# The down projection of two feed-forward blocks in seven block products instead of eight, with the affine steps on VectorE

## What is computed

```python
def _swiglu(u, w_gate, w_up, w_down):          # u 1024x1024, w_gate and w_up 1024x2816, w_down 2816x1024
    return (jax.nn.silu(u @ w_gate) * (u @ w_up)) @ w_down

def sublayer(h, j, fn, resid_w):               # shift, scale, gate: rows of mods, from c
    u = (_layer_norm(h) * (1.0 + scale) + shift).astype(h.dtype)
    z = DEEPNORM_ALPHA * h.astype(jnp.float32) + resid_w * gate * fn(u)
    return (_layer_norm(z) * ln_g[layer, j] + ln_b[layer, j]).astype(h.dtype)
```

## Time and profile before

| | us |
|---|---|
| median of 3 runs | 2212.14 (2208.69 to 2212.39) |
| the profiled execution | 2212.68 |
| its span, first to last instruction | 2210.9 |
| PE busy | 2034.5 (92%) |
| DVE busy | 1097.4 (50%) |
| ACT busy | 756.2 (34%) |
| POOL busy | 469.2 (21%) |

### The profile page before, as it was taken

How to read it: one execution, slowest core, us unless ns; L and a number is a source line. 1 busy time by engine, 2 the same in 40 slices (tenths; PEclk the granted TensorE clock), 3 DMA queues, 4 the chain that set the end, 5 groups by cost and what they waited for, 6 DMA issues and landing times. The chain is left out here.

```text
span 2210.9 us, 27004 instructions
## 1 busy us (share of the span) xinstructions
PE 2034.5 (92%) x10350; PEld 1588.2 (72%) x10350; DVE 1097.4 (50%) x1893; ACT 756.2 (34%) x1267; POOL 469.2 (21%) x336
## 2 busy tenths in 40 slices
PE   3999999999999928999889997876999999999997
PEld 2777777777888827676567775665888888878885
DVE  4854444544347483444434445567644444343656
ACT  2533323333223233434423334226433333332331
POOL 0622222220004041000023221242522222100041
PEclk7999999999999969999999999897999999999998
DMA  7253444444743122111032220604122212265341
GB/s 261 79 162 124 157 140 152 136 151 141 286 154 143 58 86 95 39 48 48 11 79 57 48 57 16 232 0 153 62 91 81 91 61 90 88 256 181 143 176 44
DMA packets 157617, 247.47 MB, mean 112 GB/s; under 512 B 8097, under 2 KB 106673, under 8 KB 157361
## 3 DMA queue, kind: packets, MB, share of 16 engines
q1 hardware_dynamic: 126370, 211.36, 27.4%
q10 hardware_dynamic: 30096, 30.25, 4.4%
q0 software_dynamic: 1024, 4.13, 1.2%
HBM read 205.09 MB, written 40.63 MB: 111 GB/s over the span
## 5 line engine op out<-in xcount | busy, mean ns | idle before, releaser
L1280 PE MATMUL f_ps<-f_uh,f_ops 128*128 128x512 f32 x2496 | 795.3, 396 | 9.1 <-DVE acc L1119 4.9
L1280 PEld LDWEIGHTS f_ps<-f_uh,f_ops 128*128 128x128 f32 x2496 | 471.3, 189 | 138.1 <-issue 28.0
L1280 PE MATMUL f_ps<-f_ul,f_ops 128*128 128x512 f32 x1248 | 491.5, 394 | 0.0
L1380 PE MATMUL f_ps<-f_wdh,f_hdh 128*128 128x512 f32 x704 | 274.1, 389 | 0.0
L1380 PE MATMUL f_ps<-f_wdl,f_hdh 128*128 128x512 f32 x704 | 273.9, 389 | 0.0
L1380 PE MATMUL f_ps<-f_wdh,f_hdl 128*128 128x512 f32 x704 | 273.9, 389 | 0.0
L1280 PEld LDWEIGHTS f_ps<-f_ul,f_ops 128*128 128x128 f32 x1248 | 235.8, 189 | 48.4
L1180 DVE TENSOR_TENSOR f_wdl<-f_wd,f_wdh 128x2048 fp32r<-128x2048 f32 x44 | 107.2, 2436 | 227.7 <-ACT f_wdh L1010 227.7
L868 POOL TENSOR_TENSOR f_sums<-f_raw 128x512 f32<-128x512 f32 x80 | 108.0, 1350 | 443.5 <-DVE f_ops L1080 341.2
L1080 DVE TENSOR_TENSOR f_ops<-f_sums,f_ops 128x512 fp32r<-128x512 f32 x160 | 117.7, 735 | 154.0 <-ACT f_ops L906 154.0
L1010 ACT CAST f_wdh<-f_wd 128x2048 fp32r<-128x2048 f32 x44 | 83.9, 1907 | 302.4 <-PE f_ps L1380 258.7
(11 more groups left out here) (214 smaller groups left out, 2671.7 us busy)
## 6 DMA issues: line engine op xcount, KB each, us to landing
f_wd<-in_ffn_w_down SPq DMA_DIRECT2D x44, 1024.0 KB, 4.9
f_raw<-in_ffn_w_gate SPq DMA_DIRECT2D x22, 1024.0 KB, 5.5
f_raw<-in_ffn_w_up SPq DMA_DIRECT2D x22, 1024.0 KB, 5.4
f_hidden<-acc SPq DMA_DIRECT2D x88, 256.0 KB, 2.2
f_hd<-f_hidden SPq DMA_DIRECT2D x44, 512.0 KB, 5.6
f_aw<-in_w_ada ACTq DMA_DIRECT2D x28, 512.0 KB, 3.5
acc<-in_w_ada ACTq DMA_DIRECT2D x28, 512.0 KB, 3.5
in_raw<-in_w_in SPq DMA_DIRECT2D x24, 512.0 KB, 3.8
```

What stands on the lines that cost most here:

```text
L1280: done = nc.tensor.matmul(ps[:, bank, :], l[:, k, :], r[:, k, :], start=fresh and k == 0 and m == 0, stop=closed and k == HK - 1 and m == ...
L1380: done = nc.tensor.matmul(ps[:, b, :], l[n % 3][:, c, P * t:P * t + P], r[n % 3][:, c, NB * (b % 2):NB * (b % 2) + NB], start=p == 0 and c ...
```

## The change

The down product is done in seven block products as well. The tokens are split into halves, and so are the output columns and, pair by pair, the hidden rows. A stage r is one block product summed over the 11 pairs (KD = 11), so there are ND = 77 steps, each with 12 matmuls: 4 token tiles by 3. Step n is pair n % 11 of stage n // 11. The stages are: 0 A11 by B11, 1 A12 by B21, 2 S2 by T2, 3 S1 by T1, 4 S4 by B22, 5 S3 by T3, 6 A22 by T4. Eight banks hold two sets of four tiles (`X_BANKS`, `Y_BANKS`), and a running sum is copied out by ScalarE where two stages share it (`copy_out`).

The sums of hidden blocks S1 to S4 are made by GpSimd in `mix_hidden`, four instructions for each pair, beside the gate and up products, and stored beside A11, A12, A22. The sums of weight blocks T1 to T3 are made by GpSimd in `mix_weights`, three for each pair, while stages 0 and 1 run. T4 is made in `fourth`, during stages 2 and 3, where stage 3 brings the block B21 once more. T3 is split early, beside stage 4 (`third_hi`, `third_lo`), so that a step of stage 5 splits only the hidden block.

Loads are 256 KB blocks in six slots; the parts lie in a ring of four (`DRING`), and those of the last steps also in four extra pairs. The last LAST = 8 steps go by tile, one tile at a time. The gate, residual, statistics, normalising, gain and shift all stand on VectorE, with the normalising fused into the gain (`affine`: two instructions of 128x1024 for tiles 0 to 3 behind steps 64 to 67, four of 128x512 for tiles 4 to 7). ScalarE's normalising and GpSimd's gain and shift are gone.

```diff
-LAST = 3
+KD = PAIRS
+ND = 7 * KD
+DSLOT = 6
+DRING = 4
+LAST = 8
...
+X_BANKS, Y_BANKS = (0, 1, 2, 6), (3, 4, 5, 7)
...
+            def load_mixed(e):
+                k = e // 2
+                if k >= 4:
+                    sp.wait_ge(tw, 3 * (k - 4) + 3)
+                if e % 2 == 0:
+                    load_down(mem.t1[k], 0, 1, k).then_inc(tw_ld[k % 4], 16)
                 else:
+                    load_down(mem.t3[k], 1, 1, k).then_inc(tw_ld[k % 4], 16)
...
+            for n in range(DSLOT, ND):
+                sp.wait_ge(d_lo, n - DSLOT + 1)
+                if stage(n - DSLOT)[0] == 3:
+                    sp.wait_ge(t4_done, stage(n - DSLOT)[1] + 1)
                 load_hidden(n)
+                load_weight(n)
+                if n < DSLOT + 2 * KD:
+                    load_mixed(n - DSLOT)
+                if n == 8:
+                    store_sums(PAIRS - 1)
...
+            def mix_hidden(q):
+                pool.wait_ge(pr, 4 * q + 4)
+                pool.wait_ge(p_st[2], 16 * (q + 1))
+                nc.gpsimd.tensor_tensor(prod(2), prod(1), prod(2), ALU.add).then_inc(mixed, 1)
...
+            def mix_weights(k):
+                t1, t2, t3 = one(mem.t1[k]), one(mem.t2[k]), one(mem.t3[k])
+                pool.wait_ge(tw_ld[k % 4], 32 * (k // 4 + 1))
+                pool.wait_ge(d_lo, k + 1)
+                nc.gpsimd.tensor_tensor(t3, t3, t1, ALU.subtract).then_inc(tw, 1)
+                pool.wait_ge(tw, 3 * k + 1)
+                nc.gpsimd.tensor_tensor(t1, t1, t2, ALU.subtract).then_inc(tw, 1)
+                pool.wait_ge(tw, 3 * k + 2)
+                nc.gpsimd.tensor_tensor(t2, t3, t2, ALU.add).then_inc(tw, 1)
...
+            def fourth(k):
+                n = 3 * KD + k
+                pool.wait_ge(d_ld[n % DSLOT], landed(n))
+                pool.wait_ge(tw, 3 * k + 3)
+                pool.wait_ge(d_lo, 2 * KD + k + 1)
+                nc.gpsimd.tensor_tensor(one(mem.t2[k]), one(mem.slots[n % DSLOT] + 1), one(mem.t2[k]),
+                                        ALU.subtract).then_inc(t4_done, 1)
...
+            def down_hi(n):
+                r, k = stage(n)
+                if later(n) >= DRING:
+                    act.wait_ge(d_mm, steps_done(n - 2 * DRING))
+                elif later(n) >= 0:
+                    act.wait_ge(d_mm, steps_done(5 * KD + 7))
+                elif n >= DRING:
+                    act.wait_ge(d_mm, steps_done(n - DRING))
...
+                act.wait_ge(d_ld[n % DSLOT], landed(n))
+                if r in (2, 3):
+                    act.wait_ge(tw, 3 * k + (3, 2)[r - 2])
+                if r == 6:
+                    act.wait_ge(t4_done, k + 1)
+                nc.scalar.copy(high_of(n), operands(n)).then_inc(d_hi, 1)
...
+            for n in range(2, ND):
+                down_lo(n)
+                for r in (1, 4, 5):
+                    if n == KD * (r + 1) + 2:
+                        for t in range(4):
+                            add_up(r, t)
+                    if n == KD * (r + 1) + 3:
+                        if r == 1:
+                            dve.wait_ge(g_half, 1)
+                        for t in range(4):
+                            weigh(r, t)
+                if 0 <= n - 4 * KD - 1 < KD:
+                    third_lo(n - 4 * KD - 1)
+                if n in (36, 37):
+                    for t in (2 * (n - 36), 2 * (n - 36) + 1):
+                        dve.wait_ge(h_ld[t], 16)
+                        residual(1, t)
...
+                if 64 <= n < 68:
+                    affine(n - 64, 1)
+                if n == 70:
+                    for t in range(4):
+                        dve.wait_ge(h_ld[4 + t], 16)
+                        residual(5, t)
+                if n == 71:
+                    for t in range(4):
+                        dve.wait_ge(d_out, 8 + t + 1)
+                        lv.half(dve, acc[:, 4 + t, :], 4 + t, 1)
...
             def down(n, tiles):
...
+                for t in tiles:
...
+                    for m in range(3):
+                        done = nc.tensor.matmul(ps[:, bank(r, t), :], left[m][:, x, P * t:P * t + P],
...
+            for n in range(ND - LAST):
+                down(n, range(4))
+            for t in range(4):
+                for n in range(ND - LAST, ND):
+                    down(n, (t,))
```

More of the change, by code:

```diff
@@ L598, in __init__ @@
             m.sb(tag + "_space", [P, D])
-        self.small = m
-        at_small, m.end = m.end, m.end + (672 if ada else 1344)
         at_l = m.end - base
@@ new lines, in store_sums, with load_hidden @@
+            def store_sums(q):
+                for n, x in enumerate((2, 1, 0, 3)):
+                    sp.wait_ge(mixed, 4 * q + n + 1)
+                    sp.dma_start(hid[(S2, S3, S1, S4)[x], q], prod(x)).then_inc(sum_st[x], 16)
+            def load_hidden(n):
+                r, k = stage(n)
+                x = (0, 3, 0, 2, 3, 1, 2)[r]
+                sp.wait_ge((p_st if r in (0, 1, 6) else sum_st)[x], 16 * (k + 1))
+                sp.dma_start(one(mem.slots[n % DSLOT]), hid[DOWN_A[r], k]).then_inc(d_ld[n % DSLOT], 16)
```

433 lines of the change are left out of this document (250 added, 183 removed).

## The result

| | median us (lowest to highest, runs) |
|---|---|
| before | 2212.26 (2208.69 to 2213.91, 4) |
| after | 2155.69 (2155.3 to 2156.83, 4) |
| ratio | 0.9745 [0.9731, 0.976] |

The forecast was 2178 us, 2154 to 2202. The direction was right and the time lies just inside the range; the gain is 56.6 us where 34 were forecast.

The account below looks back on a forecast made before the run. The prediction took TensorE's number of matmuls to bound the down product. Its terms, -29.9 + 8 + 8 + 2 - 3.5 - 1.6, gave -17.0 us per FFN, -34 for two: 2178 us, range 2154 to 2202.

Parts of the forecast that it names:

- matmuls: Down product: 132 fewer matmuls per FFN at an unchanged price of 0.227 us, 29.9 us off.
- GpSimd against VectorE: Stages 0 to 3: exclusive lock on the shared SBUF port makes TensorE wait, 8 us per FFN, bounds 0 and 14.
- VectorE's crowd at the end: Steps 64 to 76: 34.3 us of VectorE work in 26.0 us, costing 8 us per FFN, bounds 4 and 10.
- clock: TensorE's clock falls behind about three larger waits in each FFN: 2 us lost, bounds 0 and 5.
- tail: Behind the last down matmul: VectorE's remaining work falls from 12.7 to 9.2 us, 3.5 us less.
- entry: Ahead of the down product: `combine` starts earlier behind a shorter first split, 1.6 us off.
- gate and up otherwise: Gate and up products: hidden-block stores and GpSimd's `mix_hidden` beside them were costed at nothing.
- the crowd at step 24 to 26: Splits, side work and seven 1.29 us port waits: 17.2 us against 12.6 us, a TensorE wait of 4.6 us.
- The ledger of 118.5 against 114.3 us: Port work of GpSimd and VectorE up to step 42 against the time of 42 steps: short by 4.2 us.
- rival 4: Clock stays at the lower level through the waits, matmuls at half speed, 19 us per FFN lost; chance 0.02.
- Rival 3 (DMAs): Loads in stages 0 and 1 don't keep up; at 200 GB/s +9.5 us per FFN, 2231 us; chance 0.04.
- rival 1: Port costs little and clock nothing: 27 us per FFN gained, 2158 us; chance 0.15.

Follow-up runs that it names:

- experiment 5: Kernel after with GpSimd's `mix_weights` and `fourth` on 32 of 512 columns, so most weight sums are left out; 2148.6 us, ratio 0.9713.
- Experiments 6: Kernel after without the eight 128x1024 `affine` instructions of tiles 0 to 3 (gain and shift left out); 2152.5 us, ratio 0.9729.
- 11: Kernel after with side work spread and moved earlier (2147.8 us), plus stage 5's twelve weights, residuals and moments behind split 76; 2144.1 us, ratio 0.9691.
- experiments 1: Kernel before with only the small tables moved behind the large blocks of FFN memory, as in the kernel after; 2203.7 us, ratio 0.9958.
- 4: Kernel before with the gap of its small buffers made 1024 and 2048 bytes in place of 672 and 1344; 2205.4 us, ratio 0.9965.
- experiments 7: Kernel after with tiles 0 to 3 normalised on ScalarE and gain and shift on GpSimd, as before the change; 2168.1 us, ratio 0.9799.
- 12: Kernel after with side work spread and moved earlier (2147.8 us), plus only stage 5's four moments behind split 76; 2144.4 us, ratio 0.9693.

## Why the prediction was right, and what it mis-sized

Per FFN, mean of the two, with the measured value behind what the sum had:

| term | forecast | measured | from |
|---|---|---|---|
| matmuls | -29.9 | -29.9 | 132 fewer at the same price |
| GpSimd against VectorE | +8 | +3.2 | experiment 5, clock loss included |
| VectorE's crowd at the end | +8 | +8.4 | 217.8 (experiment 5) less 239.3 - 29.9, clock loss included |
| clock | +2 | in the two above | |
| tail | -3.5 | -3.4 | 12.7 to 9.3 |
| entry | -1.6 | -1.6 | wait 2.46 to 0.9 |
| gate and up otherwise | 0 | -4.9 | 6.45 less 1.6 |
| sum | -17.0 | -28.2 | |

**Matmuls, entry, tail** came out as worked out. The price stood: in the down product of after a matmul away from waits starts 0.227 us behind the one before.

**The port was the term that failed: 8 us for 3.2.** The mechanism is right: experiment 5 removes the wait with the work. The Trainium skill's exclusive lock (SBUF — State Buffer, section "SBUF: two separate sides") agrees in kind. GpSimd and then VectorE in order of time, kernel after:

```profile
576.07 1.29 POOL L994 TENSOR_TENSOR f_blocks<-f_blocks 128x512 f32<-128x512 f32 x1
577.43 2.15 POOL L996 TENSOR_TENSOR f_blocks<-f_blocks 128x512 f32<-128x512 f32 x1
```

```profile
576.18 2.26 DVE L1333 TENSOR_TENSOR f_dl<-f_blocks,f_dh 128x1024 fp32r<-128x1024 f32 x1 [1.00 <-ACT f_dh L1158]
...
596.33 0.67 DVE L1367 TENSOR_TENSOR f_ev<-f_tb,f_ps 128x512 f32<-128x512 f32 x1
596.93 1.30 DVE L1333 TENSOR_TENSOR f_dl<-f_blocks,f_dh 128x1024 fp32r<-128x1024 f32 x1
598.15 6.87 DVE L1374 TENSOR_TENSOR f_ev<-f_ev,f_gates 128x512 f32<-128x512 f32 x4
604.95 7.86 DVE L1333 TENSOR_TENSOR f_dl<-f_blocks,f_dh 128x1024 fp32r<-128x1024 f32 x4
```

The split that starts 0.11 us into a GpSimd instruction takes 2.26 us, 1.04 more than alone, and GpSimd's next one 0.86 us more. Kept until GpSimd's instruction ended it would have taken 1.18 us more; whether the port opens 0.14 us sooner, or the split does not need it in its first 0.14 us, these rows don't tell. Two of my inputs were too dear. First, I charged each of GpSimd's instructions with 1.37 us of the port and each turn with a wait of 1.29 us. The four `weigh` took 6.87 us in place of 2.49, 1.1 us of wait each, and the four splits behind them 7.86 in place of 4.7, 0.8 each. The seven waits of the crowd at step 24 to 26 made some 6 us and not 9.0; TensorE's wait there was 2.3 us for my 4.6. Second, I let GpSimd be behind all the time. `mix_weights` did its 33 instructions from 543.9 to 610.6 us, 2.02 us each, which is 1.35 in a step of 2.72 and not 1.15, and was done near step 27. From there GpSimd waited for loads between its `fourth` (12 times in the two FFNs, 20.4 us), and VectorE often found the port free. At steps 36 to 38 it did not quite: one split and the four residuals waited 4.4 us in all (629.84 to 639.0 us), half of my 9.0, and the 2.2 us on TensorE at step 37 never came. The ledger of 118.5 against 114.3 us was a sum over a time in which the demand was not even.

**VectorE's crowd: near in size, partly by luck, and incomplete in what it means.** The 8 us of the forecast were waits alone. TensorE's waits outside step 26 are 5.3 us in the first FFN and 6.1 in the second, 5.7 on average; the other 2.7 of the 8.4 are lower clock and small gaps, which the forecast had in a term of its own. By kind, the down product's excess is 1.9 us of port waits, 5.7 of other waits and 4.0 of clock and gaps, where I had 8, 8 and 2. Experiments 6 and 11 also show that taking TensorE's waits there away is worth some 1.5 to 1.8 us per FFN: VectorE itself is the bound from step 66 to the last write. The prediction treated the crowd as something that delays TensorE, with the tail behind it; the two are one queue.

**The clock cost more than I had.** The waits of the first down product are 7.6 us and all that it took over 209.4 us (239.3 less 29.9) is 12.6, so about 5.0 us are lower clock and small gaps, in the second 3.0. My 2 us (bounds 0 to 5) was low; the windows show 0.91 in the 20 us around step 26, and 0.83 in the 10 us from 720 to 730:

```profile
720.00:730.00 10.00, 9.32 (x34) 7.60 (x35) 10.00 (x15) 3.22 (x4) 0.00 (x0) 0.83 0.29 80
```

It came back 4.4 us after the wait at step 26 and 3.7 us after that at step 66, and did not fall behind the third, so rival 4 did not set in. The Trainium skill's warning (TensorE: Matmul & The Clock Gate, section "HAM oscillation — how this bites in real kernels"), a fall behind every wait, holds for two of the three large waits here.

**The gate and up products "at nothing" was wrong by 4.9 us per FFN.** The prediction put this term at nothing and gave no account of where the buffers lie. Of it 3.6 us are the layout (experiments 1 and 4: 5.4 and 1.7 us). My reading of the diff followed instructions and semaphores and passed over a line that moved a region of memory.

Another 0.8 us (1.6 in the first FFN) is a fuller clock in its first 10 us. By stretch, in experiment 1's kernel, which has it as before, and then after:

```profile
60.00:100.00 40.00, 40.00 (x188) 33.35 (x187) 30.91 (x36) 23.55 (x41) 26.91 (x17) 0.96 0.21 67
```

```profile
60.00:100.00 40.00, 40.00 (x193) 33.59 (x194) 32.52 (x37) 24.32 (x43) 27.78 (x18) 1.00 0.22 70
```

The change can't be given the credit. Of eleven traces with the gate and up code of after, eight have 473.9 or 474.0 us for this phase, and three (experiments 7, 11 and 12) have 475.5 or 475.6 with a clock of 0.83 to 0.90 from 60 to 70 us. All three traces of the older code have the lower clock, so whether the change makes it rarer stays open.

The last 0.6 us is the clock behind the entry's wait. The last product takes 2.62 us behind the wait of 0.87 us in both FFNs of after; behind the wait of 2.46 us it took 2.64 us before in the first and 3.76 in the second. The entry term had counted the wait and not the clock behind it. With 1.6 us for the wait itself this makes 8.6 and 4.4 us of the 8.6 and 4.3 measured.

**Rival 3 (DMAs)** did not occur, though it was closer than I thought. By stretch in stages 0 and 1, first FFN and second:

```profile
560.00:580.00 20.00, 20.00 (x90) 16.57 (x89) 13.55 (x8) 9.42 (x11) 19.45 (x12) 1.00 0.97 353
1945.00:1965.00 20.00, 20.00 (x90) 16.57 (x89) 11.53 (x8) 10.18 (x12) 19.52 (x10) 1.00 1.02 369
```

The DMA engines are full, and TensorE doesn't wait. The Trainium skill asks for 1 MB or more per DMA to reach three quarters of the peak, and has 341 GB/s for 1 MB (DMA: Bandwidth & Descriptors, section "Measured (HBM→SBUF, 128 partitions, SWDGE, issued from GpSimd)"). With many loads in flight this did not hold here: every DMA issued in these stretches is of 256 KB, and they stand at 353 and 369 GB/s.

The time that came out is that of rival 1 (2158 us), and of its reasons the first holds (the port cost little) and the second doesn't (the clock cost more); the layout, which no rival had, made up the difference. The two large misses, 4.8 us of the port and 4.9 us of the gate and up products per FFN, go the same way. The time stayed inside the range by 1.7 us, and that is luck.
